# One-core transformer block pair: memory places moved, two expert-weight loads requested sooner, and filling products ahead of the last expert's tiles

## The reference, cut to what matters

```python
y_a = hgrn2_mixer(...) @ w_proj_a
y_b = moba_mixer(...) @ w_proj_b
mixed = (sigmoid(gate_a) * y_a + sigmoid(gate_b) * y_b) @ w_out
x = layer_norm(DN_ALPHA * h + mixed, ln1_g, ln1_b)
ffn = hier_moe(x, ...)      # 32 experts, 2 per token
#   gate, up = split(xb @ w_gate_up[e], 2);  (silu(gate) * up) @ w_down[e]
x = layer_norm(DN_ALPHA * x + ffn, ln2_g, ln2_b)
# then second_block(x, ...)
```

## Time and profile before

| | us |
|---|---|
| median of 3 runs | 1210.22 |
| lowest and highest | 1205.82, 1211.85 |
| the profiled execution's own time | 1207.12 |
| its span in the profile | 1205.8 |
| TensorE busy in it | 1067.6 |
| VectorE, ScalarE busy | 580.0, 476.4 |
| mean granted TensorE clock, share of full | 0.945 |

### The profile page before, as it was taken

The page is one execution under the profiler, slowest core; times in us unless marked ns, Lnnn a source line. Parts: engine busy times, 40 slices in busy tenths (PEclk is TensorE's granted clock), DMA queues, the critical chain, the costliest instruction groups (busy, mean ns, idle before and its releaser), DMA issues.

```text
span 1205.8 us, 21340 instructions
## 1 busy us (share of the span) xinstructions
PE 1067.6 (89%) x9286; PEld 877.5 (73%) x9286; DVE 580.0 (48%) x851; ACT 476.4 (40%) x649; POOL 81.8 (7%) x79
## 2 busy tenths in 40 slices
PE   9999999997666676666678999999999999999998
PEld 8999898754333333333324799999999999999986
DVE  4775775733212121212112776664554548676633
ACT  5644763222111111111123744444357765544433
POOL 1640000000000000000000400000210004000000
PEclk9999999999888878888878999999999999999999
DMA  9843568999999999999999666555534236665530
GB/s 366 309 148 119 179 261 338 397 419 426 427 426 429 425 427 428 427 427 426 418 426 404 224 216 203 175 164 179 182 108 155 89 105 190 207 213 176 176 105 35
DMA packets 104220, 330.28 MB, mean 274 GB/s; under 512 B 4339, under 2 KB 76332, under 8 KB 86334
## 3 DMA queue, kind: packets, MB, share of 16 engines
q1 hardware_dynamic: 102064, 322.77, 69.7%
q10 hardware_dynamic: 1470, 4.02, 0.9%
q0 software_dynamic: 592, 2.10, 0.6%
HBM read 327.82 MB, written 1.06 MB: 273 GB/s over the span
## 4 chain that ended last, share of the span: by engine, by line
PE 64%; DMA 29%; DVE 3%; ACT 2%; issue 1%; SPq 0%; DVEq 0%; ACTq 0%
DMA wide<-in_w_gate_up_dram 22%; PE PS L488 13%; PE PS L490 12%; PE PS L489 12%; DMA wide<-in_w_down_dram 7%; PE PS L1204 5%; PE PS L835 4%; PE PS L498 2%; PE PS L499 2%; PE PS L500 2%; PE PS L829 2%; DVE lo L1962 1%; PE PS L574 1%; PE PS L815 1%; ACT hi L1452 1%
## 5 line engine op out<-in xcount | busy, mean ns | idle before, releaser
L1962 DVE TENSOR_TENSOR lo<-raw,hi 128x2048 fp32r<-128x2048 f32 (+1 forms) x111 | 253.8, 2292 | 143.4 <-ACT hi L1452 120.4
L1452 ACT CAST hi<-raw 128x2048 fp32r<-128x2048 f32 (+1 forms) x109 | 203.7, 1874 | 110.3 <-PE PS L490 75.0
L488 PE MATMUL PS<-AH,hi 128*128 128x256 f32 (+1 forms) x816 | 234.2, 287 | 1.4 <-DVE AL L2453 1.0
L489 PE MATMUL PS<-AL,hi 128*128 128x256 f32 (+1 forms) x816 | 231.4, 284 | 0.0
L490 PE MATMUL PS<-AH,lo 128*128 128x256 f32 (+1 forms) x816 | 231.4, 284 | 0.0
L835 PE MATMUL PS<-wide,XS 128*32 128x256 f32 x1568 | 128.3, 482 | 82.4 <-DMA wide<-in_w_gate_up_dram 79.1
L835 PEld LDWEIGHTS PS<-wide,XS 128*32 128x32 f32 x1568 | 56.1, 131 | 142.8 <-DMA wide<-in_w_gate_up_dram 97.2
L488 PEld LDWEIGHTS PS<-AH,hi 128*128 128x128 f32 x816 | 154.9, 190 | 3.1 <-issue 1.0
L489 PEld LDWEIGHTS PS<-AL,hi 128*128 128x128 f32 x816 | 153.7, 188 | 0.4
L490 PEld LDWEIGHTS PS<-AH,lo 128*128 128x128 f32 x816 | 153.7, 188 | 0.0
L2381 DVE TENSOR_TENSOR Y<-PS,Y 32x256 fp32r<-32x256 f32 x128 | 53.9, 421 | 125.0 <-ACT Y L1659 122.0
(11 more groups left out here) (430 smaller groups left out, 1856.4 us busy)
## 6 DMA issues: line engine op xcount, KB each, us to landing
wide<-in_w_gate_up_dram SPq DMA_DIRECT2D x49, 2048.0 KB, 45.7
wide<-in_w_down_dram SPq DMA_DIRECT2D x25, 2048.0 KB, 45.5
raw<-in_ffn_w_gate_dram SPq DMA_DIRECT2D x22, 1024.0 KB, 5.5
raw<-in_ffn_w_up_dram SPq DMA_DIRECT2D x22, 1024.0 KB, 5.7
raw<-in_w_in_dram SPq DMA_DIRECT2D x21, 1024.0 KB, 8.8
raw<-in_ffn_w_down_dram SPq DMA_DIRECT2D x19, 1024.0 KB, 5.0
spare<-in_w_gate_up_dram SPq DMA_DIRECT2D x14, 1024.0 KB, 12.7
raw<-in_sb_w_qkv_dram SPq DMA_DIRECT2D x12, 1024.0 KB, 5.2
```

The costliest lines, as they stand in the source:

```text
L488: pe.matmul(o, w(h, c), xh(k), start=start and c == c0, stop=False)
L489: pe.matmul(o, w(h, c), xl(k), start=False, stop=False)
L1452: act.copy(K.view(K.hi[i % HN], 0, [[1, n]]), K.view(K.rbuf[i], 0, [[1, n]])).then_inc(S.hi, 1)
L1962: r = e.tensor_tensor(K.view(K.lo[i % HN], 0, [[1, n]]), K.view(K.rbuf[i], 0, [[1, n]]), K.view(K.hi[i % HN], 0, [[1, n]]).bitcast(F32), A ...
```

## The change

The regions of `xtok` (now the same memory as `X1`), `OBH`/`OBL`, `LG`, `LBT`, the router's scratch (`RTR`, `ST`, `UI`, `SEL`, `SF`, `SW`, `DG`, `AI`), `HT`, `WRG`, `S12` and of some rows of the second block move to other addresses. `early8` and `early7` move forward in `ring`, to places 7 and 11, `early4` becomes place 8, and `twos` is put in an order that fits. SyncE issues `E0 + 7` with no wait, `E0 + 11` after unit 25, and the last two of the round after unit 29. `LBT` is loaded later. At the last expert three groups of five filling products come in, and `fill(4)` becomes `fill(1)`.

```diff
-    K.xtok = sb("xtok", 2048, A0 + 4 * (2048 * 3 + 1024 * 8 + 2048 + 2048))
-    K.OBH = sb("OBH", 1024, A0 + 4 * (2048 * 2 + 2048), F32R)
-    K.OBL = sb("OBL", 1024, A0 + 4 * (2048 * 2 + 3072), F32R)
+    K.OBH = sb("OBH", 1024, A0 + 72 * KB, F32R)
+    K.OBL = sb("OBL", 1024, A0 + 76 * KB, F32R)
-    K.LG = sb("LG", 1024, A0 + 92 * KB)
-    K.LBT = sb("LBT", 1024, A0 + 88 * KB)
+    K.LG = sb("LG", 1024, A0 + 97 * KB + 256)
+    K.LBT = sb("LBT", 1024, A0 + 59 * KB)
-    K.X1 = sb("X1", 2048, A0 + 56 * KB)
-    K.RTR = sb("RTR", 1024, A0 + 24 * KB)
+    K.X1 = K.xtok = sb("X1", 2048, A0 + 24 * KB)
+    K.RTR = sb("RTR", 720, A0 + 56 * KB)
...
-    ring = early[:4] + own[:3] + early[4:5] + own[3:] + early[5:]
+    ring = early[:4] + own[:3] + early[8:] + early[4:5] + own[3:5] + early[7:8] + own[5:] + early[5:7]
...
-            n = n % 10 if i < E0 + LENT else 1 + (n - (LENT - TWICE) // 2) % 6
+            n = n % 10 if i < E0 + LENT else kept[(n - (LENT - TWICE) // 2) % 6]
...
+            if e == NE - 1 and j % 2 == 0:
+                pe.wait_ge(S.ht, NE - 1)
+                fill(5, GB)
             i = K.at["gu", (e, j)]
             loaded(pe, K, S, i)
...
-    def fill(n):
+    def fill(n, b=GB + 1):
...
         if e == NE - 1:
+            fill(5, GB)
             turn(e)
         if e:
             down(e - 1)
...
         elif e == NE - 1:
             pe.wait_ge(S.ht, NE)
-            fill(4)
+            fill(1)
...
     act.dma_start(K.LG[:, :], row(t["ln1_g"])).then_inc(S.ln1, 16)
-    act.dma_start(K.LBT[:, :], row(t["ln1_b"])).then_inc(S.ln1, 16)
...
                 act.copy(view(K.MXH, c, [[1, 512]]), view(K.SGA, c, [[1, 512]])).then_inc(S.mx_hi, 1)
+    act.dma_start(K.LBT[:, :], row(t["ln1_b"])).then_inc(S.ln1, 16)
     round_hi(act, K, S, 29)
...
-    for i in range(7):
+    for i in range(8):
         sp_load(sp, K, S, K.E0 + i)

     sp.wait_ge(S.unit, 24)
-    for i in range(7, 11):
+    for i in range(8, 11):
         sp_load(sp, K, S, K.E0 + i)

-    for i in range(11, 17):
-        sp.wait_ge(S.unit, 28 + (i - 11) // 2)
+    sp.wait_ge(S.unit, 26)
+    for i in range(11, 13):
         sp_load(sp, K, S, K.E0 + i)

+    for i in range(13, 19):
+        sp.wait_ge(S.unit, 28 + (i - 13) // 2)
+        sp_load(sp, K, S, K.E0 + i)
+
     sp.wait_ge(S.unit, 30)
-    for i in range(17, 19):
+    for i in range(19, 21):
         sp_load(sp, K, S, K.E0 + i)

-    sp.wait_ge(S.x1_r, 3)
-    sp_load(sp, K, S, K.E0 + 19)
-    sp.wait_ge(S.x1_dve, 3)
-    sp_load(sp, K, S, K.E0 + 20)
```

More of the change, by code:

```diff
@@ L306, in memory @@
     K.T1 = sb("T1", 256, A0 + 101 * KB, rows=64)
-    K.HT = [sb("HT", 128, A0 + 30 * KB + 512)] * (NE - 1) + [sb("HTL", 128, A0 + 31 * KB + 64)]
-    masks = 96 * KB + 4 * CM["masks"][0]
+    K.HT = [sb("HT", 128, A0 + 62 * KB + 512)] * (NE - 1) + [sb("HTL", 128, A0 + 63 * KB + 64)]
     K.Y = sb("Y", 1024, masks, F32R)
     K.DIA = sb("DIA", 512, masks)
[L313 to L317, removed]
+    K.SEL = sb("SEL", 256, A0 + 56 * KB + 2880, F32R)
+    K.SF = sb("SF", 2 * GR, A0 + 60 * KB + 512)
+    K.SF0 = sb("SF0", 2 * GR, masks + 2048)
+    K.SW = sb("SW", 2 * GR, A0 + 61 * KB + 512)
+    K.DG = sb("DG", 8, A0 + 63 * KB)
+    K.AI = sb("AI", 128, A0 + 63 * KB + 64)
     K.PM = sb("PM", POOLW, A0 + 40 * KB + 512)
@@ L347, in memory @@
     K.AL = sb("AL", 8 * CHUNK, A0 + 10 * KB, F32R)
[L348 to L352, removed]
+    K.RS = sb("RS", L, A0 + 22 * KB + 128)
+    K.SQ1 = sb("SQ1", L, A0 + 22 * KB + 128 + 1088)
+    K.SQS = sb("SQS", L, A0 + 22 * KB + 128 + 2176)
+    K.AM = sb("AM", 128 + AW, A0 + 20 * KB)
+    K.AMR = sb("AMR", 128 + AW, A0 + 20 * KB, F32R)
     K.FH = sb("FH", 22 * L, A0 + 41 * KB, F32R)
@@ L395, in memory @@
     own = [(K.raw[i], f"raw{i}") for i in range(RN)] + [(halves[i], f"half{i}") for i in range(6)]
-    ring = early[:4] + own[:3] + early[4:5] + own[3:] + early[5:]
-    twos = [("early3", "early0"), ("raw0", "raw1"), ("raw2", "raw3"), ("raw4", "raw5"), ("half0", "half2"), ("half4", "half1"), ("half3", "half5"),
-            ("early6", "early4"), ("early2", "early7"), ("early1", "early8")]
-    at_base = (A0 + 32 * KB, 0, 16 * KB, 32 * KB, 48 * KB, 64 * KB, 80 * KB, A0 + 8 * KB, A0 + 64 * KB, A0 + 80 * KB)
+    ring = early[:4] + own[:3] + early[8:] + early[4:5] + own[3:5] + early[7:8] + own[5:] + early[5:7]
+    twos = [("early3", "early0"), ("raw0", "raw1"), ("early1", "early8"), ("raw2", "raw3"), ("early2", "early7"), ("raw4", "raw5"),
+            ("half0", "half2"), ("half4", "half1"), ("half3", "half5"), ("early6", "early4")]
+    at_base = (A0 + 32 * KB, 0, A0 + 80 * KB, 16 * KB, A0 + 64 * KB, 32 * KB, 48 * KB, 64 * KB, 80 * KB, A0 + 8 * KB)
+    kept = (1, 3, 5, 6, 7, 8)
     wide = [sb(f"wide{i}", 4096, a) for i, a in enumerate(at_base)]
@@ L922, in first_units @@
         r.then_inc(S.um_pe, 1)
-    def fill(n):
+    def fill(n, b=GB + 1):
         for _ in range(n):
-            pe.matmul(bank(GB + 1, 0, [1, 256]), con("ident"), view(K.cm, 0, [[1, 256]]), start=True, stop=True)
+            pe.matmul(bank(b, 0, [1, 256]), con("ident"), view(K.cm, 0, [[1, 256]]), start=True, stop=True)
     if e0 == 0:
@@ L2197, in group_rows @@
     iota = K.con("iota", w=GR)
-    s, f = ([view(x, GR * i, [[1, GR]]) for i in range(2)] for x in (K.SS[g % 2], K.SF))
+    s, f = ([view(x, GR * i, [[1, GR]]) for i in range(2)] for x in (K.SS[g % 2], K.SF if g else K.SF0))
     d = (lambda i, c: rt(DST + 2 * i + c, [1, 1])) if g == 0 else (lambda i, c: view(K.DG, 2 * i + c, [[1, 1]]))
@@ L2214, in group_weights @@
     iota = K.con("iota", w=GR)
-    f, w = ([view(x, GR * i, [[1, GR]]) for i in range(2)] for x in (K.SF, K.SW))
+    f, w = ([view(x, GR * i, [[1, GR]]) for i in range(2)] for x in (K.SF if g else K.SF0, K.SW))
     for i in range(2):
```

9 lines of the change are left out of this document (5 added, 4 removed).

## The result

| | before | changed |
|---|---|---|
| median of 22 runs each, us | 1205.80 | 1210.53 |
| lowest and highest | 1204.8, 1211.85 | 1206.11, 1214.75 |
| the profiled execution's own time | 1207.12 | 1213.51 |
| its span | 1205.8 | 1212.2 |
| mean granted TensorE clock | 0.945 | 0.946 |

The time after is 1.0026 [1.0015, 1.0036] times the time before, 3.1 us more. I go by the ratio. The forecast was +1.7 us and no change.

What follows compares the result with a forecast made beforehand. TensorE was taken to bound the first and second blocks, the 192 MB of weight loads the experts between. Terms -2.0 + 0.1 + 3.6 = +1.7 us on a 1210.2 us median gave 1211.9 us, range 1205.3 to 1216.0.

Steps and rivals of the forecast that it cites:

- the sum: Whole kernel: -2.0 + 0.1 + 3.6 = +1.7 us, set on the 1210.2 us median of three executions, giving 1211.9 us.
- second rival: Last expert's first fills: clock falls after TensorE rests 2.4 us; one half-clock stretch costs 1.7, total +3.4, 1213.6 us; chance 0.2.
- Part 1: Front seam, expert weight loads: two places asked for sooner gain 2.0 us, within bounds of 0 and 4.9.
- the list: Front-seam signs: 197 to 205 us over 400 GB/s, hole at 210-212, new hole 227.6-230.5, unit 21's load still near 229.
- the flow behind that hole: Front seam: after the load at 228.90 the stream flows from 230.5, ahead by 2.0 us.
- 18 places ahead of the waits: Expert loads: from 240 us on the stream is full in both kernels, so any gain there reaches the last expert.
- Part 2: ScalarE's queue before the last `w_out` rounding: loading `LBT` later costs 0.1 us, between 0 and 0.45.
- rival on `LBT`: VectorE's norm at 212.24: `LBT` lands late, at 217.3, adding 5 us for +6.7, 1216.9 us; chance 0.04.
- Part 3: Back seam, last expert: three groups of five filling products cost 3.6 us at full clock, the first waiting for `HT`.
- the forecast's tail: Back seam: TensorE followed through the new fills to the last down products, starting at 662.4 us against 658.73 before.
- the rival's upper end: Second rival with the worst of Part 2 and nothing gained in front: 5.3 + 0.45 = +5.8, 1216.0 us.
- first rival: Back seam: the three groups only take idle time, so Part 3 is 0 and the result -1.9, 1208.3 us; chance 0.25.

Runs made afterwards that it cites:

- e1: Changed kernel without its three groups of fills and with `fill(4)` again, so the front of the change alone; 0.9985 [0.9971, 0.9999] of the kernel before.
- e10: The same program as e1, run again on another chip beside e9 and e11; 0.9982 [0.9969, 0.9996] of the kernel before.
- e3: Changed kernel with its first group of fills in the other bank, waiting only for `HT` of expert 29; 0.9989 [0.9978, 1.0001] of the kernel before.
- e5: Changed kernel with its first group cut to one fill behind the same wait for `HT`; 1.0015 [1.0001, 1.0029] of the kernel before.
- e4: e1 with only `early8` moved forward in the ring, `early7` last of the round; 0.9994 [0.998, 1.0008] of the kernel before.
- e2: Kernel before with only the change's three groups of fills and `fill(1)` added; 1.0037 [1.0024, 1.005] of the kernel before, 4.5 us slower.
- e6: Changed kernel with VectorE making `HT` of expert 30 before the sums of expert 29; 0.9994 [0.9976, 1.0012] of the kernel before.
- e7: e1 plus the first group of five fills alone, in the free bank; 0.998 [0.9966, 0.9993] of the kernel before.
- e8: Changed kernel with first group free, no second group, third kept, `HT` sooner, `LBT` issued behind the last rounding; 0.9991 [0.9976, 1.0005] of the kernel before.
- e9: e7 with `LBT` issued behind the last rounding of `w_out` instead of ahead of it; 0.9979 [0.9965, 0.9992] of the kernel before.
- e11: The same program as e4, run again on another chip; 0.9987 [0.9973, 1.0002] of the kernel before.

## Why the prediction was right or wrong

**The verdict and the range: right, the closeness of the number in part luck.** No change was forecast with 0.85, 1211.9 us in 1205.3 to 1216.0. Measured were 1210.53 and +3.1 us; the sum had +1.7. The sign of both parts was right. But 1211.9 stands on a base of 1210.2, the median of three executions, and the median of 22 is 1205.8. On that base the same sum gives 1207.5, 3.0 us under what was measured, and the base was too high by 4.4: two errors that nearly cancel. The second rival (the clock falls in the first fills) had +3.4, nearer to the +3.1 than the forecast's own +1.7.

**Part 1, the mechanism right, the size somewhat off in the trace.** Every point of the list came: over 400 GB/s in 197 to 205, a hole left around 210, a new hole at 229 to 231, the load of the first place at 229.44. The term that was mis-sized is the flow behind that hole. The step set the lead at 232.5 - 230.5 = 2.0 us and took the stream as full from there on. The bytes give 1.1 to 1.2, or 0.9 to 1.6 counted from the first expert load. By the ratios the front gives 1.8 and 2.2 us (e1, e10), with intervals of 1.7 to either side: they cannot tell 2.0 from 1.1, and the size of this term stays open between the two. The step looked at unit 21 only, but 22 to 25 need their places as well: one of them is issued at 231.53 and the next after its group at 237.02, so there is a second dip at 236 (205 GB/s where the kernel before moved 434). When the stream is ahead, it could take the places of expert 0 sooner than TensorE frees them. "18 places ahead of the waits" held from 240 us on, not from 230.

**Part 2, right.** The issue cost 0.19 us where 0.1 was taken within 0 to 0.45. The landing took 8.0 us where 9.1 were counted, and the norm waits for nothing. The rival on `LBT` is out.

**Part 3, the place right, the clock wrong.** The first group waits for `HT`, as the step said, and that puts it behind the landing of the weights. Then the step took full clock, "because the nearest row has it, 0.92 over 643 to 645". In the changed kernel the row of that window says 0.50. The second rival had the outcome, a first group at half clock, but not how it came about. It said that TensorE rests 2.4 us where it rested 1.2 and comes back at half clock; the rest is there (2.31), but the clock was at 0.56 already at 641 to 642, ahead of it, under instructions that the change does not touch. In the kernel before it was the other way round: low over the down products of expert 29 (3.45 us), and back for the row of 0.92. e3, e5, e10, e4 and e2 fell as the changed kernel did, after a rest of 2.96 or 2.97 us for the same weights; e1, e6 and e7 have the order of the kernel before, after 2.15 to 2.33 us; e8, e9 and e11 had full clock over these products. So the row of 0.92 was one outcome of several. In e3, whose first group has no wait for `HT` of expert 30, TensorE was at work without a gap from 639.69 on and the clock was back at 644.4 us; in the changed kernel it stayed at 0.50 through the wait and was back at 651.4, 5.9 us after the first fill began.

The rival's price was 1.7 us for one stretch. In the trace the five fills cost 2.2 us more than the second group's 2.43, and the first pair 0.6 more than 1.93; that is 2.8 us. `HT` came 0.8 us sooner than counted (645.5 for 646.3), and the forecast's tail of 22.2 us (640.2 to 662.4) became 24.6. By the ratio of e2 the part costs 4.5 us, between the forecast's 3.6 and the 5.3 that the rival's upper end uses. That 5.3 is 3.6 and the 1.7 us of one stretch at half clock (3.60 less 1.93 in the earlier trace rows, with a granted clock of 0.52 in the earlier trace rows); no run shows it as such, and what e2 shows is 6.1 us more in the tail and 4.5 by the ratio. A cost of 4.5 us would fit executions of both kinds; the two that were profiled with the wait and all five fills (the changed kernel and e2) paid the clock.

What the runs show of fills and the clock is this. In the five profiled kernels with the second group ahead of it (the changed one, e2, e3, e5, e6) the second pair took 1.93 or 1.94 us; in seven of the eight without it (the kernel before, e1, e7 to e11) 2.69 to 3.64, and 1.93 in e4. After how much work the clock comes back they do not settle: it was back after 5.9 us without a gap in the changed kernel, and after 12, almost without one, in e10 (last section). The first group stood behind the rest that it should have bridged, and was itself run at a granted clock of 0.50.

**What the prediction did not see** is which part of the term mattered. Its sum sets all fifteen products in line, at 0.45 us each, and takes off the 1.7 us of clock and three of the old fills. e3 has all fifteen and costs nothing that can be told from e1. For comparison, e1 waits 1.11 and 2.27 us for the two pairs and has the second one at half clock (3.64); e3 waits for neither and has it in 1.94. So most of the fills take the room of waits and of half clock that are there anyway, as the first rival said, once the wait for `HT` is gone. (That rival counted 3.5 us of waits, with one in `fill(4)`; the earlier trace rows show no idle time there, and 2.3 us in all.) I read this so: the first rival was right on the second and third group, the second rival on the first, and the sum of part 3 came near the measured cost because the full price of the two free groups stood in for the half clock of the first.

**Left open:** how the cost of the first group (4.0 to 4.5 us by the ratios) divides between the wait and the clock; why the clock fell in some executions under the same instructions and not in others; whether the second place in front is worth more than nothing; whether the free first group is.

## What to carry to other kernels

A filling product must be free to run in the very gap that it should fill: a wait for another engine's semaphore ahead of it, or a bank that is still in use, turns it into work behind the gap, and here five of them took 4.63 us at a granted clock of 0.50, where later groups took 2.43 and 2.32. Loads that are requested sooner are ahead only until the ring has gone round once (here 4.8 us at 215 us, 1.1 at 240), so count when the first places are freed, and not the first alone but as many as the stream would take while it is ahead. Where TensorE has rests, do not take the clock of a stretch from the one row that stands there in the kernel before: the same products of expert 29 took 1.93 to 3.52 us in these runs. Cost the stretch at both levels, a granted clock of 1.00 and of 0.50.

## What the runs showed of the hardware that was not expected

**One stage, two speeds, at full granted clock.** The feed-forward stages of the second block run at one of two speeds in an execution, and not by the kernel: e4 and e11 are one program, and the first stage (740 to 800 us) has 476 instructions in the one and 489 in the other. Windows of the kernel before:

```profile
740.00:800.00 60.00, 60.00 (x489) 60.00 (x488) 37.78 (x32) 25.13 (x20) 0.00 (x0) 1.00 0.55 178
1080.00:1130.00 50.00, 50.00 (x427) 50.00 (x426) 32.40 (x29) 21.65 (x19) 0.00 (x0) 1.00 0.59 200
```

and of the changed kernel:

```profile
740.00:800.00 60.00, 60.00 (x476) 60.00 (x475) 36.24 (x29) 24.35 (x21) 0.00 (x0) 1.00 0.57 176
1080.00:1130.00 50.00, 50.00 (x443) 50.00 (x443) 32.44 (x28) 24.29 (x19) 0.00 (x0) 1.00 0.58 187
```

TensorE is busy for the whole of each, the clock is 1.00, and yet the first has 489 or 476 instructions and the second 443 or 427. In e3 both stages are quick and 545.1 us lie behind the last down products; in e6 and e7 both are slow and 549.8 to 550.0 do; with one slow stage it is 547.1 to 547.6. So each slow stage costs about 2.4 us, which is much of the scatter that a change of this size has to be seen through. Its cause is open.

**Half clock through 12 us of work.** e10 has no new fills, and its TensorE timeline shows

```profile
645.49 3.64 PE L836 MATMUL PS<-wide,XS 128*32 128x256 f32 x32 [3.36 <-DMA wide<-in_w_gate_up_dram]
...
652.61 3.64 PE L836 MATMUL PS<-wide,XS 128*32 128x256 f32 x32
```

where e1, the same program, rested 1.11 us before its first pair and had it in 1.94. The two tails differ by 1.9 us. The rest of 3.36 us did not bring the clock down: it was at 0.50 from 641 us on, ahead of it, and stayed there until 657.5 us, through 12 us of work (from 645.49 on) almost without a gap. In e1 it was low ahead of the rest of 1.11 us and back before it (1.00 over 643 to 645), and the pair behind ran at full clock. So a tail read from one profile is uncertain by about 2 us.
